# First 42 expert blocks of the first PEER pass: both activation parts in one 512-column matmul, their sum on VectorE, and the gate stage nine blocks later

## The chip, the cores and the metric

The kernel runs on one core of a Trainium2 chip. The metric is the device time of one launch in microseconds (us); lower is better. Three runs of the kernel before gave 1034.63, 1034.99 and 1036.53 us, median 1034.99. In the text PE is TensorE (PEld its weight loads), DVE is VectorE, ACT is ScalarE, POOL is GpSimd and SP is the engine that issues the weight DMAs.

## The reference, cut to what matters

One decoder layer for 256 tokens and a model width of 1024: attention in two head groups, then PEER, a retrieval of 16 of 128 x 128 single-neuron experts per head for 8 heads, and a final norm. The change touches PEER alone:

```python
s1, s2 = q1 @ keys1, q2 @ keys2                 # (T, 8, 128) each
v1, i1 = top_k(s1, 16); v2, i2 = top_k(s2, 16)
cand = v1[..., :, None] + v2[..., None, :]      # 16 x 16 sums per head
sc, ci = top_k(cand, 16)
e = i1[ci // 16] * 128 + i2[ci % 16]            # which experts
g = softmax(sc)
act = gelu(hc @ exp_u[e])                       # hc: (T, 1024)
out = (g * act) @ exp_v[e]
```

The kernel computes it densely: gelu(h · u) for all 16384 experts in 128 blocks of 128 experts, each multiplied by a gate that is zero for experts that weren't chosen, and then the product with all of v.

## The kernel before

**Split numbers.** Each fp32 factor is split into a high part that the matmul takes exactly and a low part, the rest. A product takes three of the four combinations: high·high, high·rest, low·high. `h2r[:, 0]` holds the high part of the activations h (128 rows, 8 chunks of the contraction, 256 tokens) and `h2r[:, 1]` the rest; the weights of a block are `hi_t` and `lo_t`.

**The first pass (u pass).** `u_block(n)`, for n from 0 to 127, computes 128 experts by 256 tokens in half a PSUM bank, banks 4 and 5 in turn. For each of 8 chunks two matmuls of 256 columns take the same weights `hi_t` with both activation parts (L875, L876); then 8 matmuls of 256 columns take `lo_t` with the high part (L879). A block so has 24 matmuls of 256 columns. The second pass (v pass, L899 and L906) has 12 matmuls of 512 columns a block.

**Who feeds a block.** SP loads block n into one of 5 raw buffers once block n-5 is done. ACT copies it into `hi_t` (L591, 3 buffers, so not before block n-3 is done). The low part is raw minus high: on POOL for n below `POOL_LOW` = 46 (L434), on DVE from there on (L1231). ACT also takes the gelu of the finished block from PSUM (L612 or L610). ACT's order in the loop is `high(n + 1)`, then `gelu(n - 1)`: so `high(k + 3)` stands right behind `gelu(k)`, and an engine runs its instructions in the order in which they are written. Block n+2 waits for the gelu of block n to free its bank.

**The sort.** While PE runs the first 46 blocks, DVE finds the 16 best of each list. For each of two tiles of 128 tokens: `top16` over 16 lists of 128 scores (MAX8 L1185, FIND_INDEX8 L1188, MATCH_REPLACE8 L1192, and again for the next 8), the candidate sums (L1203), `top16` over 8 lists of 256, the difference to the best (L1207, after which ACT may take the exponential, at its step `EXP_AT` = 38), and twice a comparison, a product and a reduction over 2048 columns, `hit` and `chosen` (L1217, L1219, L1221), which look the chosen indices up. Then come the gate sums and `chosen_ready` (L1226).

**The gates.** Before block `TURN_AT` = 46 PE waits for `chosen_ready` and transposes the choices (L934). From block `GATE_AT` = 52 on, each of 64 blocks is preceded by the matmuls that build the gates of 4 tokens (L890, 8 matmuls) out of one-hot rows that DVE makes (L1242 to L1248). DVE multiplies them into the activations of all blocks done so far (L1259), ACT keeps the rest of them for the blocks to come (L619), and `late` (L1267) multiplies these in later. The last gates so stand ahead of block 115, and 12 blocks without gates follow before the v pass.

## Time and profile before

| | before |
|---|---|
| median of 3 runs | 1034.99 us |
| profiled execution | 1034.67 us, its span 1032.9 us |
| u pass on PE | 266.4 to 674.1 us |
| PE, DVE, ACT, POOL busy | 93%, 72%, 47%, 27% of the span |
| granted TensorE clock | 0.973 of full speed over the span |

The span runs from the first instruction to the last; some 1.8 us of the execution lie outside it. The groups further down come from the page, from the chain that ended last (each piece follows the one that released it), from the instructions of an engine in order of time (start, duration, engine and line, result and operands with shapes, count, and in brackets the idle time before and who ended it), and from stretches of time with each engine's busy time. Two instructions on an engine overlap by some 0.07 us where the second needs nothing of the first, so durations of neighbours add up to a little more than the time between starts.

### The profile page before, as it was taken

The page shows a single profiled execution, that of the slowest core. Times are in us where ns is not written, and L with a number is a line of the kernel's source. Part 1 is how long each engine was busy: PE and PEld are TensorE (multiplying, and loading weights), DVE is VectorE, ACT ScalarE, POOL GpSimd, SP SyncE. Part 2 cuts the span into 40 slices and gives each one's busy share as a digit, 9 for nine tenths or more (in the row PEclk, how much of TensorE's full clock was granted, in tenths as well). Part 3 has the DMA queues.
Part 4 walks back from the last instruction along what each step waited for, and adds up shares of the span by engine and source line. Part 5 has one row for each costly group of instructions (what it writes and reads, how often), then busy time and mean ns, then how long its engine had stood idle before and what let it go on. Part 6 is the DMA issues. An engine that isn't in the chain of part 4 may idle for free.

```text
span 1032.9 us, 16975 instructions
## 1 busy us (share of the span) xinstructions
PE 960.8 (93%) x6674; PEld 881.5 (85%) x6674; DVE 740.6 (72%) x1358; ACT 486.9 (47%) x865; POOL 278.7 (27%) x138
## 2 busy tenths in 40 slices
PE   2299898699999999999999999999999999999996
PEld 2198778698999999999999999988888888888884
DVE  4935869870699998789999998555555555555555
ACT  5355435332644454454444444454545454545453
POOL 5566446656799995000000000000000000000000
PEclk9599999899999999999999999999999999999998
DMA  9994457612365665554545545666666666666662
GB/s 291 285 363 168 164 202 328 265 62 103 102 184 165 183 184 165 164 160 149 163 149 158 156 152 164 184 183 195 193 195 193 195 192 193 194 193 195 193 194 102
DMA packets 58162, 191.60 MB, mean 186 GB/s; under 512 B 4946, under 2 KB 23522, under 8 KB 56932
## 3 DMA queue, kind: packets, MB, share of 16 engines
q1 hardware_dynamic: 58018, 190.50, 57.3%
q8 instruction: 53, 0.87, 0.4%
q14 instruction: 25, 0.20, 0.1%
q0 software_dynamic: 64, 0.03, 0.0%
q10 hardware_dynamic: 2, 0.00, 0.0%
HBM read 189.44 MB, written 1.07 MB: 184 GB/s over the span
## 4 chain that ended last, share of the span: by engine, by line
PE 82%; DVE 9%; POOL 4%; ACT 2%; issue 1%; DMA 1%; SPq 0%; DVEq 0%; ACTq 0%
PE banks L899 22%; PE banks L906 11%; PE banks L875 11%; PE banks L879 11%; PE banks L876 10%; PE banks L720 5%; DVE acc L962 5%; POOL lo L434 4%; PE banks L890 3%; PE banks L729 2%; PE banks L717 1%; DMA sc_w<-in_w_ada 1%; PE banks L726 1%; DVE prob L1085 1%; PE banks L857 1%
## 5 line engine op out<-in xcount | busy, mean ns | idle before, releaser
L1231 DVE TENSOR_TENSOR lo<-raw,hi 128x1024 fp32r<-128x1024 f32 x210 | 258.9, 1233 | 169.7 <-ACT hi L591 168.3
L591 ACT ACTIVATE hi<-raw 128x1024 fp32r<-128x1024 f32 x256 | 271.5, 1061 | 169.7 <-PE banks L906 169.7
L875 PE MATMUL banks<-h2r,hi 128*128 128x256 f32 x1024 | 256.4, 288 | 0.0
L899 PE MATMUL banks<-hi,wsplit 128*128 128x512 f32 x1024 | 253.2, 389 | 0.5 <-DVE wsplit L1272 0.5
L876 PE MATMUL banks<-h2r,hi 128*128 128x256 f32 x1024 | 251.1, 283 | 0.0
L899 PEld LDWEIGHTS banks<-hi,wsplit 128*128 128x128 f32 x1024 | 192.2, 188 | 40.5 <-issue 0.7
L876 PEld LDWEIGHTS banks<-h2r,hi 128*128 128x128 f32 x1024 | 196.6, 192 | 0.0
L875 PEld LDWEIGHTS banks<-h2r,hi 128*128 128x128 f32 x1024 | 196.0, 191 | 0.0
L879 PE MATMUL banks<-h2r,lo 128*128 128x256 f32 x1024 | 143.9, 283 | 3.4 <-POOL lo L434 3.4
L906 PE MATMUL banks<-lo,wsplit 128*128 128x512 f32 x512 | 137.0, 389 | 0.0
L879 PEld LDWEIGHTS banks<-h2r,lo 128*128 128x128 f32 x1024 | 132.0, 192 | 4.2 <-POOL lo L434 4.2
L434 POOL TENSOR_TENSOR lo<-raw,hi 128x1024 fp32r<-128x1024 f32 x46 | 129.4, 2836 | 20.5 <-ACT hi L591 20.1
L906 PEld LDWEIGHTS banks<-lo,wsplit 128*128 128x128 f32 x512 | 96.1, 188 | 19.9
L610 ACT ACTIVATE gelu_out<-banks 128x256 f32<-128x256 f32 (+32 forms) x75 | 22.1, 295 | 131.7 <-PE banks L879 131.7
L612 ACT ACTIVATE act<-banks 128x256 f32<-128x256 f32 (+31 forms) x116 | 37.4, 323 | 84.1 <-PE banks L879 84.1
L427 POOL TENSOR_TENSOR win_low<-win,high 128x1024 fp32r<-128x1024 f32 x24 | 59.3, 2494 | 40.1 <-ACT high L462 40.1
L1272 DVE TENSOR_TENSOR wsplit<-act,wsplit 128x256 fp32r<-128x256 f32 x128 | 53.4, 417 | 0.4 <-ACT wsplit L631 0.4
L631 ACT ACTIVATE wsplit<-act 128x256 fp32r<-128x256 f32 x128 | 51.2, 400 | 0.0
L1248 DVE TENSOR_TENSOR oh2g<-oh,part_h 128x512 f16<-128x512 f16 x128 | 48.2, 417 | 0.0
L427 POOL TENSOR_TENSOR wq_low<-wq,high 128x1024 fp32r<-128x1024 f32 x16 | 40.7, 2575 | 23.0 <-ACT high L462 23.0
L962 DVE SCALAR_TENSOR_TENSOR acc<-sc_w,cact,acc 128x256 f32<-128x256 f32 (+1 forms) x35 | 39.9, 1141 | 1.1
L890 PE MATMUL banks<-oh2g,oh 128*128 128x128 f16 x512 | 40.6, 220 | 0.0
(171 smaller groups left out, 1057.8 us busy)
## 6 DMA issues: line engine op xcount, KB each, us to landing
raw<-in_u_t SPq DMA_DIRECT2D x128, 512.0 KB, 3.6
raw<-in_v_b SPq DMA_DIRECT2D x128, 512.0 KB, 3.8
win<-in_w_in SPq DMA_DIRECT2D x8, 1024.0 KB, 11.9
g_w<-in_w_ada SPq DMA_DIRECT2D x2, 4096.0 KB, 14.3
wq<-in_wq SPq DMA_DIRECT2D x2, 4096.0 KB, 13.7
sh_w<-in_w_ada SPq DMA_DIRECT2D x4, 1024.0 KB, 11.9
sc_w<-in_w_ada SPq DMA_DIRECT2D x4, 1024.0 KB, 12.1
win<-in_w_in SPq DMA_DIRECT2D x1, 4096.0 KB, 19.1
```

Of the source, the lines that this page charges most:

```text
L427: nc.gpsimd.tensor_tensor(low_of[name][:, :, c], full[name][:, :, c], high_slot(w)[:, :, e * P:(e + 1) * P].bitcast(F32), ALU.subtract).th ...
L434: nc.gpsimd.tensor_tensor(lo_t[n % RAW][:, :], raw[n % RAW][:, :], hi_t[:, n % HI, :].bitcast(F32), ALU.subtract).then_inc(pool_low, 1)
L591: nc.scalar.activation(hi_t[:, n % HI, :], raw[n % RAW][:, :], ACT.Copy).then_inc(high_ready, 1)
L875: nc.tensor.matmul(dst, w, h2r[:, 0, c, :], start=(c == 0), stop=False)
L876: nc.tensor.matmul(dst, w, h2r[:, 1, c, :], start=False, stop=False)
L879: last = nc.tensor.matmul(dst, lo_t[n % RAW][:, c * P:(c + 1) * P], h2r[:, 0, c, :], start=False, stop=(c == DC - 1))
L890: last = nc.tensor.matmul(bank[g_bank(g)][:, k * KEYS:(k + 1) * KEYS], oh1[:, g % 2, k // PT, :, k % PT], oh2g[:, g % 2, e, k // PT, :, k ...
L899: nc.tensor.matmul(bank[2 * t + half][:, :], wsplit[:, j % WS, e, t * P:(t + 1) * P], hi_t[:, n % HI, half * 512:half * 512 + 512], start= ...
L906: last = nc.tensor.matmul(bank[2 * t + half][:, :], wsplit[:, j % WS, 0, t * P:(t + 1) * P], lo_t[n % RAW][:, half * 512:half * 512 + 512] ...
L962: ins = nc.vector.scalar_tensor_tensor(out=dst, in0=w[:, c, :], scalar=cact[:, c:c + 1], in1=dst, op0=ALU.mult, op1=ALU.add)
L1231: nc.vector.tensor_tensor(lo_t[n % RAW][:, :], raw[n % RAW][:, :], hi_t[:, n % HI, :].bitcast(F32), ALU.subtract).then_inc(vector_low, 1)
L1272: nc.vector.tensor_tensor(wsplit[:, j % WS, 1, :], act[:, j, :], wsplit[:, j % WS, 0, :].bitcast(F32), ALU.subtract).then_inc(wl_ready, 1)
```

## The change

For the first `MERGED` = 42 blocks, the two matmuls of 256 columns with the same weights become one of 512 columns: the high products go into columns 0 to 255 of a bank and the products with the rest into columns 256 to 511. The low weights still add to columns 0 to 255. A DVE `tensor_reduce` adds the two halves of a block into `u_sum` (two buffers, in SBUF), and ACT takes the gelu from there; it waits for this sum (`summed`) where it waited for the block. Four banks take the blocks in turn, so that block n waits for the sum of block n-4. The sum of block n waits for the block and for the gelu of block n-2.

The sums stand inside DVE's sort at fixed places. `weave` adds up the sort's lengths by numbers in the code (0.2, 0.27, 0.33, 0.4, 2.3, 2.4 and 4.4 us for its instructions, 0.65 for a sum) and puts sum k in as soon as the total is over 3.0 · (k + 1.4). `EXP_AT` goes from 38 to 45, `POOL_LOW` and `TURN_AT` from 46 to 55 (POOL makes nine more low parts and DVE nine fewer) and `GATE_AT` from 52 to 61, so that the last gates stand ahead of block 124.

```diff
-EXP_AT = 38
-POOL_LOW = 46
-TURN_AT = 46
-GATE_AT = 52
+EXP_AT = 45
+POOL_LOW = 55
+TURN_AT = 55
+GATE_AT = 61
+MERGED = 42
...
+        def u_bank(n):
+            return (4, 5, 0, 1)[n % 4] if n < MERGED else 4 + n % 2
...
             def gelu(n):
                 before = gated_before(n)
+                if n < MERGED:
+                    sc.wait_ge(summed, n + 1)
+                    nc.scalar.activation(act[:, n, :], u_sum[:, n % 2, :], ACT.Gelu).then_inc(act_out, 1)
+                    return
                 sc.wait_ge(block_used, n + 1)
...
             def u_block(n):
                 pe.wait_ge(high_ready, n + 1)
-                if n >= 2:
-                    pe.wait_ge(act_out, n - 1)
+                if n < MERGED:
+                    if n == 2:
+                        pe.wait_ge(rows_read, 3)
+                    if n >= 4:
+                        pe.wait_ge(summed, n - 3)
+                    for c in range(DC):
+                        nc.tensor.matmul(bank[u_bank(n)].rearrange("p (e s) -> p e s", e=2),
+                                         hi_t[:, n % HI, c * P:(c + 1) * P], h2r[:, :, c, :],
+                                         start=(c == 0), stop=False, skip_group_check=True)
+                    low_ready(n)
+                    for c in range(DC):
+                        last = nc.tensor.matmul(bank[u_bank(n)][:, 0:SEQ], lo_t[n % RAW][:, c * P:(c + 1) * P],
+                                                h2r[:, 0, c, :], start=False, stop=(c == DC - 1), skip_group_check=True)
+                    last.then_inc(block_used, 1)
+                    return
+                pe.wait_ge(act_out, n - 1)
...
+            SLOT = 3.0
+            sorted_for, added = [0.0], [0]
+            def add_parts(n):
+                ve.wait_ge(block_used, n + 1)
+                if n >= 2:
+                    ve.wait_ge(act_out, n - 1)
+                nc.vector.tensor_reduce(u_sum[:, n % 2, :], bank[u_bank(n)].rearrange("p (e s) -> p s e", e=2), AX.X,
+                                        ALU.add).then_inc(summed, 1)
+            def weave(length):
+                sorted_for[0] += length
+                while added[0] < MERGED and SLOT * (added[0] + 1.4) < sorted_for[0]:
+                    add_parts(added[0])
+                    added[0] += 1
+                    sorted_for[0] += 0.65
...
                         last = nc.vector.max(vals[:, l, k:k + 8], src(l))
+                        if l < n - 1:
+                            weave(one)
...
                     link(nc.vector.tensor_tensor(hit[:, :, :, :], hit[:, :, :, :],
                                                  spread(halves_i[:, half], 2, TOPK), ALU.mult))
+                    weave(4.4)
                     link(nc.vector.tensor_reduce(chosen[:, t, half, :], hit[:, :, :, :], AX.X, ALU.add))
+                    weave(2.3)
```

On PE, in the fourth and fifth block (n = 3 and 4), the order of the changed kernel is this (L887 takes `hi_t`, L892 takes `lo_t`):

```order
337 L887 MATMUL banks<-h2r,hi 128x512 [waits high_ready]
338 L887 MATMUL banks<-h2r,hi 128x512 x7
339 L892 MATMUL banks<-h2r,lo_107 128x256 [waits pool_low]
340 L892 MATMUL banks<-h2r,lo_107 128x256 x7
341 L887 MATMUL banks<-h2r,hi 128x512 [waits summed,high_ready]
342 L887 MATMUL banks<-h2r,hi 128x512 x7
343 L892 MATMUL banks<-h2r,lo_108 128x256 [waits pool_low]
344 L892 MATMUL banks<-h2r,lo_108 128x256 x7
```

A block has 16 matmuls in place of 24, and from n = 4 on it waits for a sum. On DVE, the last part of the second tile's sort, from the comparison on, before:

```order
187 L1217 TENSOR_TENSOR hit<-part,iota 128x2048
188 L1219 TENSOR_TENSOR hit<-hit,top_i 128x2048
189 L1221 TENSOR_REDUCE chosen<-hit 128x128
190 L1217 TENSOR_TENSOR hit<-part,iota 128x2048
191 L1219 TENSOR_TENSOR hit<-hit,top_i 128x2048
192 L1221 TENSOR_REDUCE chosen<-hit 128x128
```

And the same part in the changed kernel, where L1214 is the sum of a block's halves, L1270 the comparison, L1273 the product and L1276 the reduction:

```order
249 L1270 TENSOR_TENSOR hit<-part,iota 128x2048
250 L1214 TENSOR_REDUCE u_sum<-banks 128x256 x2
251 L1273 TENSOR_TENSOR hit<-hit,top_i 128x2048
252 L1214 TENSOR_REDUCE u_sum<-banks 128x256
253 L1276 TENSOR_REDUCE chosen<-hit 128x128
254 L1270 TENSOR_TENSOR hit<-part,iota 128x2048
255 L1273 TENSOR_TENSOR hit<-hit,top_i 128x2048
256 L1276 TENSOR_REDUCE chosen<-hit 128x128
```

These three sums are the last ones, of blocks 39, 40 and 41: the last sum stands four long instructions ahead of the sort's end. At the start of the sort the first sums stand here (L1229 is MAX8, L1234 FIND_INDEX8):

```order
149 L1229 MAX top_v<-score 128x8 x16
150 L1234 MAX_INDEX top_iu<-top_v,score 128x8 x5
151 L1214 TENSOR_REDUCE u_sum<-banks 128x256
152 L1234 MAX_INDEX top_iu<-top_v,score 128x8 x9
153 L1214 TENSOR_REDUCE u_sum<-banks 128x256
```

Before, the 16 searches for indices stood there without a break.

## Rows read from the trace of the kernel before

**Rows 1.** The page: busy time by engine, chain that ended last by engine.

```profile
PE 960.8 (93%) x6674; PEld 881.5 (85%) x6674; DVE 740.6 (72%) x1358; ACT 486.9 (47%) x865; POOL 278.7 (27%) x138
...
PE 82%; DVE 9%; POOL 4%; ACT 2%; issue 1%; DMA 1%; SPq 0%; DVEq 0%; ACTq 0%
```

**Rows 2.** The chain in order of time (start us, us, what), 255 to 480 us.

```profile
268.56 0.96 PE banks L879 x8
...
271.44 0.96 PE banks L879 x8
...
373.97 19.66 POOL lo L434 x5
...
402.56 0.96 PE banks L879 x8
403.52 0.66 PE banks L934 x6
...
421.44 0.48 PE banks L890 x8
```

**Rows 3.** The chain on PE in the second pass, 674 to 690 us.

```profile
677.14 1.81 PE banks L899 x8
678.95 0.91 PE banks L906 x4
```

**Rows 4.** DVE's instructions in order of time (start us, us, engine, line), first tile's sort.

```profile
267.10 3.19 DVE L1185 MAX8 top_v<-score 128x8 f32<-128x128 f32 x16 [18.04 <-ACT score L596]
270.32 0.09 DVE L1188 MATCH_VALUE_LOAD top_iu<-top_v,score 128x8 f32 x1
...
286.48 1.44 DVE L1200 CAST top_i<-top_iu 128x256 f32<-128x256 uint32 x1
...
305.65 2.43 DVE L1207 TENSOR_TENSOR gate<-best 128x128 f32<-128x128 f32 x1
```

**Rows 5.** The same, last part of the second tile's sort.

```profile
371.39 4.38 DVE L1217 TENSOR_TENSOR hit<-part,iota 128x2048 f32<-128x2048 f32 x1
375.80 4.39 DVE L1219 TENSOR_TENSOR hit<-hit,top_i 128x2048 f32<-128x2048 f32 x1
380.23 2.29 DVE L1221 TENSOR_REDUCE chosen<-hit 128x128 f32<-128x2048 f32 x1
...
391.42 2.29 DVE L1221 TENSOR_REDUCE chosen<-hit 128x128 f32<-128x2048 f32 x1
```

**Rows 6.** DVE groups by shape (busy us, mean ns): reduce of two kinds.

```profile
L1221 DVE TENSOR_REDUCE chosen<-hit 128x128 f32<-128x2048 f32 x4 | 9.1, 2286 | 0.1
...
L1073 DVE TENSOR_REDUCE nmax<-logit 128x2 f32<-128x512 f32 x8 | 5.5, 686 | 0.3
```

**Rows 7.** DVE in order of time, late in the gate window.

```profile
629.86 0.62 DVE L1259 TENSOR_TENSOR act<-banks,act 128x452 f32<-128x452 f32 x1
630.41 1.23 DVE L1231 TENSOR_TENSOR lo<-raw,hi 128x1024 fp32r<-128x1024 f32 x1
...
633.26 0.62 DVE L1259 TENSOR_TENSOR act<-banks,act 128x456 f32<-128x456 f32 x1
```

**Rows 8.** ACT in order of time, from the first block.

```profile
269.56 0.38 ACT L612 ACTIVATE act<-banks 128x256 f32<-128x256 f32 x1 [1.06 <-PE banks L879]
269.84 1.05 ACT L591 ACTIVATE hi<-raw 128x1024 fp32r<-128x1024 f32 x1
```

**Rows 9.** POOL in order of time.

```profile
305.53 2.40 POOL L434 TENSOR_TENSOR lo<-raw,hi 128x1024 fp32r<-128x1024 f32 x1 [0.48 <-ACT hi L591]
```

**Rows 10.** PE in order of time, after the first tile's hit products.

```profile
330.99 1.22 PE L879 MATMUL banks<-h2r,lo 128*128 128x256 f32 x8 [1.25 <-POOL lo L434]
```

**Rows 11.** PE in order of time, its longest wait in the attention stage.

```profile
117.04 0.61 PE L778 MATMUL banks<-ident,prob 128*128 128x128 f32 x2 [4.04 <-DVE prob L1085]
```

**Rows 12.** Stretches: busy us (count) of each engine, then PEclk, DMA share, GB/s.

```profile
112.00:118.00 6.00, 1.96 (x15) 1.43 (x13) 5.89 (x6) 1.93 (x2) 6.00 (x3) 0.93 1.10 437
118.00:122.00 4.00, 4.00 (x26) 3.78 (x25) 3.96 (x4) 0.95 (x5) 1.19 (x1) 0.68 0.91 393
```

More of the change, by code:

```diff
@@ L153, in hybrid_peer_layer @@
         gelu_out = at("gelu_out", M0 + 1024, [P, 2, SEQ])
+        u_sum = at("u_sum", M0 + 1024, [P, 2, SEQ])
         iota_t = at("iota_t", M0, [P, GQ, KEYS, PT], F16)
@@ L239, in hybrid_peer_layer @@
             sem, ("second_ready", "onehot_ready", "gates_ready", "gates_used", "gates_out"))
+        summed = sem("summed")
         wh_ready, wl_ready, peer_ready, x2_ready, final_ready = map(
@@ L1178, in _, with top16 @@
                                     None, ALU.mult).then_inc(rows_read, 1)
-            def top16(vals, idx, src, n):
+            SLOT = 3.0
[12 more added lines that the diff above has]
+                    sorted_for[0] += 0.65
+            def top16(vals, idx, src, n, one):
                 for k in range(0, TOPK, 8):
@@ L1188, in top16 @@
                         last = nc.vector.max_index(idx[:, l, k:k + 8], vals[:, l, k:k + 8], src(l))
+                        if l < n - 1:
+                            weave(one + 0.07)
                     link(last)
@@ L1192, in top16 @@
                             last = nc.vector.match_replace(src(l), vals[:, l, k:k + 8], src(l), -3.0e38)
+                            if l < n - 1:
+                                weave(one + 0.07)
                         link(last)
@@ L1198, in _ @@
                     ve.wait_ge(s_ready, TT * LISTS // 4)
-                top16(top_v, top_iu, lambda l: score[:, t, l, :], LISTS)
+                top16(top_v, top_iu, lambda l: score[:, t, l, :], LISTS, 0.2)
                 link(nc.vector.tensor_copy(top_i[:, :, :], top_iu[:, :, :]))
@@ L1204, in _ @@
                                              spread(halves_v[:, 1], 2, TOPK), ALU.add))
-                top16(best, best_iu, lambda h: cand[:, h, :, :].rearrange("p a b -> p (a b)"), HEADS)
+                weave(2.3)
+                top16(best, best_iu, lambda h: cand[:, h, :, :].rearrange("p a b -> p (a b)"), HEADS, 0.33)
                 nc.vector.tensor_tensor(gate[:, t, :, :], best[:, :, :],
@@ L1209, in _ @@
                                         ).then_inc(gate_max, 1)
+                assert added[0] <= EXP_AT
+                weave(2.4)
                 nc.vector.tensor_scalar(part_u[:, 0, :, :], best_iu[:, :, :], 4, None, ALU.logical_shift_right)
@@ L1218, in _ @@
                                                  ALU.is_equal))
+                    weave(4.4)
                     link(nc.vector.tensor_tensor(hit[:, :, :, :], hit[:, :, :, :],
                                                  spread(halves_i[:, half], 2, TOPK), ALU.mult))
+                    weave(4.4)
                     link(nc.vector.tensor_reduce(chosen[:, t, half, :], hit[:, :, :, :], AX.X, ALU.add))
+                    weave(2.3)
             ve.wait_ge(gate_exp, TT)
@@ L1275, in _ @@
             low(POOL_LOW)
+            assert added[0] == MERGED, added
             low(POOL_LOW + 1)
```

## The prediction

> **What bounds the kernel now.** I read the page first. PE is busy 93% of the span, and 82% of the chain that ended last is PE [rows 1]: whatever shortens or stops PE shows in the time. Then the chain in order of time. In the u pass the low products of two blocks start at 268.56 and 271.44, so a block takes 2.88 us, and its 8 low matmuls take 0.96 us, 0.12 us each [rows 2]; 16 high ones are 1.92 us. Block 0 ends at 269.52 (268.56 + 0.96) and block 45, the last before the transposes, at 403.52. These are 134.0 us for 45 blocks, where 45 x 2.88 = 129.6: PE lost 4.4 us. The chain says to whom: five of POOL's low parts from 373.97 on took 19.66 us, 3.93 each [rows 2], while one of them usually takes 2.40 [rows 9]; PE's wait at 330.99 is the end of the earlier such period [rows 10]. Last, DVE in order of time tells why. A product of 2048 columns with both inputs in SBUF takes 4.4 us beside a busy POOL, the gate difference of only 128 columns 2.43 us and a cast of 256 columns 1.44 [rows 4, 5]: such an instruction and POOL's take turns, some 2.2 us of waiting for each other and 2.2 of work. A reduction of 2048 columns takes 2.29 us in the same stretch [rows 5], so it does not take part in the turns.
>
> The Trainium skill says the same of this pair in "SBUF — State Buffer", section "Who interferes with whom": a tensor_tensor with two SBUF inputs shuts GpSimd out of a shared port for its whole length and the other way round, and on trn2 a tensor_reduce never does; by that rule, with which the trace agrees, the 42 new sums cost POOL nothing.
>
> **What the change saves on PE.** In the v pass 8 matmuls of 512 columns take 1.81 us, 0.227 each [rows 3], against 0.240 for two of 256. A merged block is 1.81 + 0.96 = 2.77 us in place of 2.88. For 42 blocks that is 42 x 0.11 = 4.6 us, if nothing else holds a block up.
>
> "TensorE: Matmul & The Clock Gate", section "Wait — 56ns, not 53.3ns?", of the Trainium skill puts a warm matmul at its columns over 2.4 GHz and 2.5 ns; by that the merge would save 0.02 us a block, 0.9 us in all. The trace's 0.120 and 0.227 are both above it, and the rows give the larger gain.
>
> **What it adds on DVE.** 42 sums, each reading 512 columns of PSUM. A reduction of 512 columns took 0.686 us, and one of 2048 took 2.29, so it is the columns read that count [rows 6]. A PSUM read with a stride, 452 columns, took 0.62, and the next instruction started 0.55 after it [rows 7]: neighbours overlap by 0.07. So a sum takes 0.62 of DVE's time and ends 0.69 after its start. Bounds: 0.55, that row's distance, and 1.10, if the alternating halves went at the pace of L1217, 4.38 us for 2048 columns [rows 5]. I take 0.62, since both nearer rows stand there. 42 sums make 26 us on an engine that had no pause in the sort.
>
> **Where this lands.** The sums stand at fixed places of the sort, so DVE's progress through the sort now sets when a block is released. Behind the sum of block k stand in a row: its gelu (the copy after it starts 0.28 later), ACT's copy for block k+3 (1.05) [rows 8], and POOL's low part of k+3 (2.40) [rows 9]; 3.8 us with the hand-overs. Block k+3 wants its low part 2 x 2.77 + 1.81 = 7.35 us after the end of block k. The sum may thus end 3.5 us after its block; later than that, PE waits. The wait for the sum of block n-4 is looser by a block and never decides.
>
> Sum 0 stands behind 16 MAX8, done at 270.32 [rows 4], and five searches, so it starts over 2 us after block 0. Sum 39 stands behind the comparison that ended at 371.39 + 4.38 = 375.77 [rows 5]. With 39 sums ahead of it, 39 x 0.62 = 24.2, it ends at 375.77 + 24.2 + 0.69 = 400.6. From the first to the 39th that is about (400.6 - 270.3) / 40 = 3.3 us a sum, where a block used to take 2.88 and would take 2.77. PE uses up its 3.5 us in some three blocks and then goes at DVE's pace. The gain of 4.6 us so lies beside a wait and is worth nothing here; the 4.4 us that were lost to POOL lie inside the new waits too.
>
> Now the walk from sum 39 at 400.6, by the order of instructions:
> - gelu 39, then ACT's copy 42 until 402.0. DVE does sum 40 and then finds the port free (POOL waits for the copy): product 401.3 to 403.45.
> - POOL's low part 42 from 403.45 to 405.85, block 42 ends 0.96 + 0.1 later, 406.9. Sum 41 is done at 404.1, the reduction at 406.4.
> - low part 43 until 408.25; block 43 (unmerged again) ends at 409.8.
> - DVE's third comparison takes the port from 408.25 to 410.4, low part 44 until 412.8, block 44 ends at 413.8.
> - the last product 412.8 to 414.95, low part 45 until 417.35, block 45 ends at 418.3.
>
> Before, block 45 ended at 403.52 [rows 2]: **14.8 us later**. From there each block takes 2.88 as before.
>
> Three corrections to DVE's stream ahead of sum 39:
> - *DVE waits for PE.* Where long instructions stand (cast and candidates; gate difference and comparison, in both tiles) some 7 us pass between sums, and PE falls back by about 4 us. The next sums stand in pairs or close together, but their blocks aren't done: DVE waits. An engine that is late for its partner in one stretch and early in the next loses on both sides. Four such places, half a block (1.25) lost at each: +5.0. Bounds 0 and a block at each, 11.
> - *Port time given back.* POOL, held up by PE's pace, is now busy 44 x 2.40 = 106 of some 135 us, 78%. The part of DVE's waits for it that falls away is 22% of 16.5 us (five products and comparisons at 2.2, two gate differences at 2.2, a cast at 1.1 [rows 4, 5]): -3.6. Bounds 0 and -16.5.
> - *PE's clock.* In the kernel before, PE waited 4.04 us at one place [rows 11]; the granted clock was 0.93 of full speed in the 6 us around it and 0.68 in the next four [rows 12], which is 4 x 0.32 = 1.3 us of full-speed work. In the u pass it was never paused that long. The four new pauses of about 4 us are of this size; I count one of them, +1.3. Bounds 0 and 5.2.
>
> **What the rest costs.** The exponential at ACT's step 45 stands where the kernel before had it at 38, behind a value that DVE has long made; it delays copies that have 3.5 us to spare: 0, up to 2. POOL's nine more low parts replace DVE's: 0 on PE, since 2.40 fits in 2.88. `chosen_ready` comes some 5 us after the sort, near 422, and the transposes now stand ahead of block 55, at 418.3 + 9 x 2.88 = 444: no wait. The 64 gate groups are the same (8 matmuls in 0.48 [rows 2]). But their last ones now meet longer rows: DVE's round between two gate products was 3.40 us (629.86 to 633.26 [rows 7]), which is PE's 2.88 + 0.48 and the hand-over, with DVE full; 36 more columns add 0.04 a round for the last seven, and only three blocks follow instead of twelve before the v pass needs wsplit: +0.3, between 0 and 2.
>
> Sum: 14.8 + 5.0 - 3.6 + 1.3 + 0.3 = 17.8. On the profiled execution, 1034.67, that makes 1052.5 us; the median of the runs is 0.3 above this execution, which I leave in the range.
>
> **The rivals.**
> - *PE sets the pace after all (faster).* One mechanism: DVE's sort with its sums keeps within 3.5 us of the blocks, and the merge pays. For it: the numbers of the weave ask for 3.0 us a sum, near a block. Against it: these leave out the cast's and the link instructions' time and DVE's stream, summed from rows, runs at 3.3. It needs the stream ahead of sum 39 shorter by some 18 us, more than all of DVE's waits for the port. Price: -4.6, 1030.1 us. By the skill's matmul times quoted above it would be 1033.8.
> - *The port is given back nearly whole.* POOL idles whenever DVE asks. -16.5 for -3.6: 1039.6; half of it, 1046. For it: POOL will always wait for ACT's copy. Against it: it also must catch up after each pause, just when DVE's long products stand.
> - *The clock falls at each pause.* 3 x 1.3 more and waits of DVE behind it: 1056 to 1062. For it: the one wait of 4.04 us. Against: PE's pause is broken by the high products, which start before the low part is there.
> - *Nothing changes*, because savings on PE and port cancel the pace: 1035. It would need sum 39 near 385.
>
> **How the numbers follow.** The forecast holds 0.70, for 1047 to 1058; the clock 0.12; the port 0.11; faster 0.05; no change 0.02. The likeliest gives 1052.5. For 8 in 10 the range takes in the forecast's own, half of the port's rival and most of the clock's: 1045 to 1061. A sum at 1.10 us, 20 us more, is left outside. What a measurement can tell from no change is 0.2%, 2 us: faster 0.05, within 0.02, slower 0.93.
>
> **What would show it.** The profile after should show: 16 matmuls a block, 0.227 and 0.120 us; sums of 0.69; ACT's gelu waiting for DVE in most of the first 42 blocks; PE waiting for ACT's copy or POOL's low part near the casts and products, some 20 us in all; block 41 done near 404 to 408 and block 45 near 418 to 421; v pass unchanged but 18 us later. I am wrong if the gelus find their sums ready, if the waits lie at the turn to the v pass, or if a sum takes the time of L1217.

## The result, and the profile after

| | before | after |
|---|---|---|
| median (range), the same chip | 1035.76 us (1034.63 to 1038.09, 4 runs) | 1055.10 us (1054.90 to 1055.73, 4 runs) |
| profiled execution, its span | 1034.67, 1032.9 | 1055.28, 1053.5 |
| first matmul of the u pass to first of the v pass | 266.41 to 674.13: 407.7 | 268.04 to 694.72: 426.7 |
| granted clock over the span | 0.973 | 0.965 |

The ratio is 1.0185, 95% interval 1.0165 to 1.0204: 1.9% slower, clear of no change. The u pass is 19.0 us longer. The other 1.6 us between the two spans lie ahead of the u pass, and the experiments show starts between 266.3 and 268.7 whatever the edit, so they are not the change's. Two lines of the page, busy time and the chain by engine, answer to [rows 1]:

```profile
PE 967.8 (92%) x6338; PEld 869.3 (83%) x6338; DVE 750.1 (71%) x1382; ACT 486.2 (46%) x865; POOL 291.5 (28%) x147
...
PE 72%; DVE 19%; POOL 3%; ACT 2%; issue 2%; DMA 1%; SPq 0%; DVEq 0%; ACTq 0%
```

DVE's busy time grew by only 9.5 us, but its share of the chain went from 9% to 19%: it did not become full, it is waited for. The v pass kept its length (its high matmuls start from 674.1 to 1021.7 us before, from 694.7 to 1042.3 after). Here are PE's instructions of the u pass that come after its longer waits (start, duration, what, idle before and who ended it):

```profile
297.85 3.78 PE L887 MATMUL banks<-h2r,hi 128*128 128x512 f32 x8 [3.38 <-ACT hi L598]
325.55 2.14 PE L887 MATMUL banks<-h2r,hi 128*128 128x512 f32 x8 [2.43 <-ACT hi L598]
329.17 1.22 PE L892 MATMUL banks<-h2r,lo 128*128 128x256 f32 x8 [1.49 <-POOL lo L441]
...
379.99 2.11 PE L887 MATMUL banks<-h2r,hi 128*128 128x512 f32 x8 [3.00 <-ACT hi L598]
408.50 0.35 PE L900 MATMUL banks<-h2r,hi 128*128 128x256 f32 x1 [3.61 <-ACT act L613]
422.89 1.22 PE L904 MATMUL banks<-h2r,lo 128*128 128x256 f32 x8 [1.24 <-POOL lo L441]
```

All 13 waits from 266 to 430 add up to 18.3 us; before, there were four of 3.4 us in all, one of them in [rows 10]. The first matmuls after a wait tell the clock: 8 of 512 columns took 3.78 us at 297.85, and 2.14 and 2.11 at the next two such places. The stretches (the columns are those of [rows 12]) show where full speed was lost:

```profile
291.00:314.00 23.00, 19.54 (x95) 16.47 (x95) 22.49 (x72) 8.10 (x12) 15.56 (x7) 0.85 0.43 129
314.00:344.00 30.00, 25.75 (x143) 21.46 (x141) 26.91 (x26) 12.54 (x20) 24.11 (x9) 1.00 0.54 157
...
394.00:423.00 29.00, 22.90 (x146) 20.28 (x146) 28.69 (x29) 13.93 (x22) 22.48 (x9) 0.94 0.43 140
```

That is 23 x 0.15 + 29 x 0.06 = 5.2 us of full-speed work; about 0.5 of it lies in the pause ahead of 297.85, whose last 0.95 us already had the lower clock (0.50 granted from 296.90 on). The chain that ended last, in the stretch that answers to [rows 2], no longer runs over PE's own matmuls but over DVE's instructions, a copy of ACT and POOL's low parts:

```profile
403.63 2.30 DVE hit L1270
...
405.96 0.70 DVE u_sum L1214
...
407.00 1.05 ACT hi L598
...
408.12 14.72 POOL lo L441 x4
```

The groups of the new sums, and of the gelus behind them (busy us, mean ns, idle before and until whom), answer to [rows 6, 8]:

```profile
L1214 DVE TENSOR_REDUCE u_sum<-banks 128x256 f32<-128x512 f32 x42 | 28.3, 680 | 5.9 <-PE banks L892 4.9 <-DVE chosen L1276 0.7
L613 ACT ACTIVATE act<-u_sum 128x256 f32<-128x256 f32 x42 | 17.5, 417 | 84.5 <-DVE u_sum L1214 84.5
```

Both directions of the coupling stand there: ACT waited 84.5 us for sums, and DVE in turn 4.9 us for blocks. Nearly all of the 4.9 lies at two sums:

```profile
330.43 0.69 DVE L1214 TENSOR_REDUCE u_sum<-banks 128x256 f32<-128x512 f32 x1 [2.81 <-PE banks L892]
...
349.10 0.69 DVE L1214 TENSOR_REDUCE u_sum<-banks 128x256 f32<-128x512 f32 x1 [1.84 <-PE banks L892]
```

Last, DVE in order of time, the instructions beside the sums, which answer to [rows 4, 5]:

```profile
291.70 1.65 DVE L1250 CAST top_i<-top_iu 128x256 f32<-128x256 uint32 x1
...
315.62 0.29 DVE L1258 TENSOR_TENSOR gate<-best 128x128 f32<-128x128 f32 x1
315.83 0.68 DVE L1214 TENSOR_REDUCE u_sum<-banks 128x256 f32<-128x512 f32 x1
316.43 1.93 DVE L1263 TENSOR_SCALAR part_u<-best_iu 128x128 uint32<-128x128 uint32 x1
318.29 2.44 DVE L1264 TENSOR_SCALAR part_u<-best_iu 128x128 uint32<-128x128 uint32 x1
...
321.08 2.29 DVE L1270 TENSOR_TENSOR hit<-part,iota 128x2048 f32<-128x2048 f32 x1
...
324.62 2.28 DVE L1273 TENSOR_TENSOR hit<-hit,top_i 128x2048 f32<-128x2048 f32 x1
...
333.96 4.41 DVE L1270 TENSOR_TENSOR hit<-part,iota 128x2048 f32<-128x2048 f32 x1
...
339.60 3.17 DVE L1273 TENSOR_TENSOR hit<-hit,top_i 128x2048 f32<-128x2048 f32 x1
...
373.08 2.42 DVE L1250 CAST top_i<-top_iu 128x256 f32<-128x256 uint32 x1
...
397.39 0.62 DVE L1258 TENSOR_TENSOR gate<-best 128x128 f32<-128x128 f32 x1
...
398.54 2.38 DVE L1263 TENSOR_SCALAR part_u<-best_iu 128x128 uint32<-128x128 uint32 x1
400.84 2.43 DVE L1264 TENSOR_SCALAR part_u<-best_iu 128x128 uint32<-128x128 uint32 x1
```

Four long instructions of the first tile that took 4.4 us before now take between 2.28 and 4.41, but in each tile two small ones of 128 columns, which follow a sum, take 1.9 to 2.4. In the kernel before, the same two and the second tile's cast read:

```profile
308.00 0.21 DVE L1210 TENSOR_SCALAR part_u<-best_iu 128x128 uint32<-128x128 uint32 x1
308.13 0.21 DVE L1211 TENSOR_SCALAR part_u<-best_iu 128x128 uint32<-128x128 uint32 x1
...
350.43 0.29 DVE L1200 CAST top_i<-top_iu 128x256 f32<-128x256 uint32 x1
...
368.45 2.31 DVE L1207 TENSOR_TENSOR gate<-best 128x128 f32<-128x128 f32 x1
```

### The profile page after: what moved, and what is told of

It reads as the page before. It is cut to its first block, busy times and chain, and to the rows that moved or that the text cites. A ratio compares the mean times of both kernels' runs of the same rounds, so it can differ in the third digit from the quotient of the medians.

```text
span 1053.5 us, 16356 instructions
## 1 busy us (share of the span) xinstructions
PE 967.8 (92%) x6338; PEld 869.3 (83%) x6338; DVE 750.1 (71%) x1382; ACT 486.2 (46%) x865; POOL 291.5 (28%) x147
## 4 chain that ended last, share of the span: by engine, by line
PE 72%; DVE 19%; POOL 3%; ACT 2%; issue 2%; DMA 1%; SPq 0%; DVEq 0%; ACTq 0%
PE banks L924 22%; PE banks L931 11%; PE banks L900 8%; PE banks L904 7%; PE banks L901 7%; PE banks L731 5%; DVE acc L987 5%; POOL lo L441 3%; PE banks L915 3%; PE banks L740 2%; DVE u_sum L1214 2%; DVE top_iu L1234 2%; PE banks L728 1%; DMA sc_w<-in_w_ada 1%; DVE top_v L1229 1%
## 5 line engine op out<-in xcount | busy, mean ns | idle before, releaser
L1287 DVE TENSOR_TENSOR lo<-raw,hi 128x1024 fp32r<-128x1024 f32 x201 | 246.2, 1225 | 182.0 <-ACT hi L598 180.5
L900 PE MATMUL banks<-h2r,hi 128*128 128x256 f32 x688 | 174.6, 292 | 3.6 <-ACT act L613 3.6
L901 PE MATMUL banks<-h2r,hi 128*128 128x256 f32 x688 | 169.3, 284 | 0.0
L441 POOL TENSOR_TENSOR lo<-raw,hi 128x1024 fp32r<-128x1024 f32 x55 | 141.6, 2595 | 51.0 <-ACT hi L598 51.0
L900 PEld LDWEIGHTS banks<-h2r,hi 128*128 128x128 f32 x688 | 132.0, 192 | 3.8 <-ACT hi L598 3.8
L901 PEld LDWEIGHTS banks<-h2r,hi 128*128 128x128 f32 x688 | 132.5, 193 | 0.0
L887 PE MATMUL banks<-h2r,hi 128*128 128x512 f32 x336 | 86.5, 400 | 8.8 <-ACT hi L598 8.8
L904 PEld LDWEIGHTS banks<-h2r,lo 128*128 128x128 f32 x688 | 89.2, 193 | 2.5 <-POOL lo L441 2.5
L887 PEld LDWEIGHTS banks<-h2r,hi 128*128 128x128 f32 x336 | 61.7, 193 | 20.6 <-ACT hi L598 9.4
L621 ACT ACTIVATE gelu_out<-banks 128x4 f32<-128x4 f32 (+32 forms) x66 | 18.7, 283 | 119.6 <-PE banks L904 119.6
L613 ACT ACTIVATE act<-u_sum 128x256 f32<-128x256 f32 x42 | 17.5, 417 | 84.5 <-DVE u_sum L1214 84.5
L892 PEld LDWEIGHTS banks<-h2r,lo 128*128 128x128 f32 x336 | 45.7, 193 | 11.4 <-POOL lo L441 8.9
L892 PE MATMUL banks<-h2r,lo 128*128 128x256 f32 x336 | 48.8, 289 | 4.3 <-POOL lo L441 4.1
## 6 DMA issues: line engine op xcount, KB each, us to landing
g_w<-in_w_ada SPq DMA_DIRECT2D x2, 4096.0 KB, 15.2
```

What stands on the lines that cost most here:

```text
L441: nc.gpsimd.tensor_tensor(lo_t[n % RAW][:, :], raw[n % RAW][:, :], hi_t[:, n % HI, :].bitcast(F32), ALU.subtract).then_inc(pool_low, 1)
L887: nc.tensor.matmul(bank[u_bank(n)].rearrange("p (e s) -> p e s", e=2), hi_t[:, n % HI, c * P:(c + 1) * P], h2r[:, :, c, :], start=(c == 0) ...
L892: last = nc.tensor.matmul(bank[u_bank(n)][:, 0:SEQ], lo_t[n % RAW][:, c * P:(c + 1) * P], h2r[:, 0, c, :], start=False, stop=(c == DC - 1) ...
L900: nc.tensor.matmul(dst, w, h2r[:, 0, c, :], start=(c == 0), stop=False)
L901: nc.tensor.matmul(dst, w, h2r[:, 1, c, :], start=False, stop=False)
L904: last = nc.tensor.matmul(dst, lo_t[n % RAW][:, c * P:(c + 1) * P], h2r[:, 0, c, :], start=False, stop=(c == DC - 1))
```

## The experiments

Each kernel ran beside the kernel before on its chip; the medians of before there were 1035.6 (n1 to n3, n5), 1035.5 (n4, n6 to n8), 1035.0 (n9 to n11) and 1035.1 us (n12). "u pass" is the distance between the first matmuls of the two passes: 407.7 before, 426.7 after.

| run | median us | ratio to before, 95% | u pass |
|---|---|---|---|
| n1 constants alone | 1036.1 | 0.9990 to 1.0013 | 407.7 |
| n2 merged, no sums | 1033.7 | 0.9969 to 0.9989 | 405.6 |
| n3 sums of half the columns | 1046.0 | 1.0082 to 1.0119 | 418.0 |
| n4 sums every 2.7 | 1041.9 | 1.0041 to 1.0071 | 414.4 |
| n5 copy ahead of gelu | 1049.9 | 1.0120 to 1.0162 | 421.6 |
| n6 both of these | 1037.1 | 1.0001 to 1.0021 | 409.0 |
| n7 also true lengths, 36 merged | 1034.8 | 0.9986 to 1.0003 | 407.4 |
| n8 DVE's load, nobody waits | 1032.8 | 0.9953 to 0.9977 | 404.8 |
| n9 before, lookup in PSUM | 1030.4 | 0.9948 to 0.9973 | 403.3 |
| n10 merged, lookup in PSUM | 1038.9 | 1.0028 to 1.0059 | 411.5 |
| n11 after, lookup in PSUM | 1050.3 | 1.0131 to 1.0160 | 423.6 |
| n12 n10 with sums every 2.5 | 1029.1 | 0.9923 to 0.9948 | 400.7 |

Two single executions stand far out, 1597 us in n6 and 3331 us of the kernel before beside n12; nothing on record explains them, and the medians don't hang on them.

**n1, the four constants alone.** The kernel before with only this part of the change:

```diff
-EXP_AT = 38
-POOL_LOW = 46
-TURN_AT = 46
-GATE_AT = 52
+EXP_AT = 45
+POOL_LOW = 55
+TURN_AT = 55
+GATE_AT = 61
```

> The kernel before with only the four numbers of the change: the exponential at step 45, POOL's low parts and the transposes up to block 55, the gates from block 61. No merged matmuls and no sums. My theory (the loss is DVE's pace in the sort) puts these at +0.3 us, 0 to 2: 1036.1 us, v pass starting 0 to 0.5 us later than in the kernel before. Rival: the later gates run into the turn to the v pass, or POOL's nine more low parts hold PE up; then this run shows 5 us or more of the 19, with PE waits near the last gates or in blocks 46 to 55.

The u pass kept its 407.7 us and the median is within what can be told. The later gates and POOL's nine more low parts cost nothing; all of the loss is in the merged blocks.

**n2, merged without sums.** The gelu reads the high half straight from the bank, so the product with the activations' rest is left out for 42 blocks:

```diff
-                    sc.wait_ge(summed, n + 1)
-                    nc.scalar.activation(act[:, n, :], u_sum[:, n % 2, :], ACT.Gelu).then_inc(act_out, 1)
+                    sc.wait_ge(block_used, n + 1)
+                    nc.scalar.activation(act[:, n, :], bank[u_bank(n)][:, 0:SEQ], ACT.Gelu).then_inc(act_out, 1)
...
-                        pe.wait_ge(summed, n - 3)
+                        pe.wait_ge(act_out, n - 3)
...
-                    add_parts(added[0])
```

> The changed kernel without DVE's sums: the gelu of the first 42 blocks reads the high half of the bank and waits for the block as before; the products with the rest of the activations are made but not added. My theory: PE then runs 42 blocks at 2.77 us and the time is the kernel before's less 42 x 0.11 = 4.6 plus 0.3 for the constants: 1031.5 us, with the two periods of POOL's slow low parts (4.4 us) as before or up to 1.5 us larger, since PE is faster. Rival: 512-column matmuls over two halves cost what the sums seem to cost (weights or PSUM): then it stays above 1040.

Half of the gain that I expected: the u pass is 2.1 us shorter, not 4.3. The chain in order of time shows why the first half is smaller:

```profile
268.15 1.85 PE banks L887 x8
269.99 0.95 PE banks L892 x8
270.95 1.84 PE banks L887 x8
```

A merged block takes 2.79 us, 0.230 a matmul, so 42 of them save 3.8. Most of the rest is POOL: PE's four waits for it, of 0.90, 1.32, 0.81 and 1.25 us, remain (4.3 us with 3.4 before), and two more blocks were held up by 0.3 each. I take it that a quicker PE runs into POOL's slow periods earlier; no run shows that by itself.

**n8, DVE's load without the coupling.** n2 with 42 reductions of the same size and at the same places, but of columns in SBUF that are long ready, and nobody waits for them:

```diff
-                ve.wait_ge(block_used, n + 1)
-                    ve.wait_ge(act_out, n - 1)
-                nc.vector.tensor_reduce(u_sum[:, n % 2, :], bank[u_bank(n)].rearrange("p (e s) -> p s e", e=2), AX.X,
+                    ve.wait_ge(summed, n - 1)
+                nc.vector.tensor_reduce(u_sum[:, n % 2, :], xs[:, 0, 0:512].rearrange("p (e s) -> p s e", e=2), AX.X,
```

> The changed kernel with 42 reductions of 512 columns on DVE at the same places, but of columns in SBUF that are ready, waiting for no block, and with nobody waiting for them; the gelu takes the high half of the bank as in the kernel without sums (the products with the rest of the activations are not added). DVE's load as in the changed kernel, the coupling gone. Theory (coupling): the sort ends some 25 us later, near 424, still ahead of the transposes near 440: 1033.7, up to 1 more. Rival (DVE's load itself, by the port it shares with POOL or the late choice): 1040 or more.

42 reductions of 696 ns on DVE, 29 us, cost nothing. What costs in the changed kernel is not DVE's time, but that PE must wait for the place at which a sum stands. These reductions read SBUF, so the run doesn't test whether reads of the PSUM banks cost anything; n12 does, with 42 such reads and a single wait of PE, 0.75 us.

**n3, half of a sum's columns.** The sum covers 128 of 256 tokens, and the gelu uses it for both halves (the others' product is left out):

```diff
-                nc.vector.tensor_reduce(u_sum[:, n % 2, :], bank[u_bank(n)].rearrange("p (e s) -> p s e", e=2), AX.X,
+                nc.vector.tensor_reduce(u_sum[:, n % 2, 0:P], bank[u_bank(n)].rearrange("p (e s) -> p s e", e=2)[:, 0:P, :], AX.X,
```

> The changed kernel with each sum over 128 of the 256 tokens, at the same place; the gelu takes these for both halves of the tokens, so the output of the other half is not computed. A sum takes 0.33 us of DVE's time in place of 0.60. Theory of DVE's stream: 42 x 0.27 = 11 us less work ahead of the last sum, of which DVE's waits for PE give back a part: 8 to 11 us faster than the changed kernel, 1044 to 1047. Rival (the long instructions between two sums and the chain behind a sum make the loss, not the sums' own time): 0 to 3 us faster, 1052 to 1055.

A sum took 0.412 us instead of 0.680, 11.3 us less in 42, and the u pass fell by 8.7 us: the time follows DVE's stream, less what DVE then waits more for PE (8.3 us in place of 4.9).

**n4, the sums closer together.** The sums stand at the same work, earlier in the sort:

```diff
-            SLOT = 3.0
+            SLOT = 2.7
-                while added[0] < MERGED and SLOT * (added[0] + 1.4) < sorted_for[0]:
+                while added[0] < MERGED and SLOT * (added[0] + 1.1) < sorted_for[0]:
```

> The changed kernel with the sums placed closer: sum k at 2.7 (k + 1.1) of the sort's counted length in place of 3.0 (k + 1.4). The same 42 sums, the same ACT order. Theory (what counts is how much sort stands ahead of each sum): the last sum has 13.5 us of counted sort less ahead of it, DVE waits a little more for PE in exchange: 7 to 12 us faster than the changed kernel, 1043 to 1048. Rival (the number of sums, or DVE's load, sets the loss): 1054 to 1056.

12.3 us less for two numbers, without any work removed; the median, 1041.9, is 1.1 us below the range that I gave. The pauses that ACT's copy ended are 1.00, 0.93 and 1.04 us long, and the clock is at full speed behind them:

```profile
298.26 2.12 PE L887 MATMUL banks<-h2r,hi 128*128 128x512 f32 x8 [1.00 <-ACT hi L598]
...
385.26 2.10 PE L887 MATMUL banks<-h2r,hi 128*128 128x512 f32 x8 [1.04 <-ACT hi L598]
```

Of the 6.7 us that n4 still loses against the kernel before, only 2.8 stand at the end of block 45. The others lie behind it, where the last lookups now meet POOL's low parts and PE waited for POOL three times (1.13, 0.74 and 1.25 us).

**n5, ACT's copy ahead of the gelu.** `high(k + 3)` stands ahead of `gelu(k)`, so a late sum doesn't hold up the copy behind it:

```diff
-                if HI <= n + 1 < STREAM:
-                    high(n + 1)
+                ahead = n + 2 if n <= MERGED else n + 1
+                if HI <= ahead < STREAM and n != MERGED + 1:
+                    high(ahead)
```

> The changed kernel with ACT's copy for block k+3 ahead of the gelu of block k for the first 42 blocks, so that a late sum no longer holds the copy and POOL's low part; a sum then holds PE only through its bank, a block and the chain's 3.8 us later. Theory: the pauses at the four places with long instructions shrink from about 4 us to 1 or less, but DVE's stream still brings the last sum to 402 to 405: 4 to 8 us faster than the changed kernel, 1047 to 1051. If DVE's stream alone were the bound, and the order on ACT did nothing: 1055. If the chain behind the sum alone were: back to 1035 or below.

5.1 us shorter, as expected in size; the pauses did only half of what I expected. The slack of a sum grew, and two of them shrank, from 3.38 and 3.00 us to 1.61 and 0.19. But the second one grew from 2.43 to 3.22, and with DVE's stream nearly as long as before, PE met it at the end of the merged blocks:

```profile
404.42 0.55 PE L901 MATMUL banks<-h2r,hi 128*128 128x256 f32 x1 [6.36 <-ACT act L613]
```

**n6, n4 and n5 together.**

> Both at once: ACT's copy for block k+3 ahead of gelu k, and the sums at 2.7 (k + 1.1). Theory: the two act on different parts, the placing on DVE's stream, the order on the pauses at the long instructions, so most of both adds up: 1036 to 1041. PE's pauses should be under 2 us each. Rival (both remove the same wait): no better than the better of the two alone, 1043 to 1050.

The u pass is 409.0 us, 17.7 less than after, where the two alone gave 12.3 and 5.1: they add up. One makes the sums come faster, the other widens the time that PE can do without one.

**n7, and with the true lengths.** n6 with the cast's and the small instructions' time counted in the weave, 0.61 for a sum and 36 merged blocks:

```diff
                 link(nc.vector.tensor_copy(top_i[:, :, :], top_iu[:, :, :]))
+                weave(1.5)
...
                 link(nc.vector.tensor_copy(part[:, :, :, :], part_u[:, :, :, :]))
+                weave(0.8)
...
-                    sorted_for[0] += 0.65
+                    sorted_for[0] += 0.61
-MERGED = 42
+MERGED = 36
```

> The previous edit, with the sort's lengths counted as the trace has them (1.5 for the cast and 0.8 for the three small ones that the weave leaves out, 0.61 for a sum) and 36 merged blocks in place of 42, so that the last sums stand ahead of the second tile's long products. Theory: a sum then comes within what its block can wait for, and the time falls to that of the kernel without sums (1033.7) plus at most 3: 1033.5 to 1036.5, same as the kernel before or just faster. Rival (some wait for DVE remains at each long instruction whatever the placing): 1038 or more.

All of the loss is gone, and of the gain 0.4 us show. At the end of block 45 the whole gain of 36 merged blocks was there: 133.87 us from the first matmul, 3.25 less than before, with waits of 0.31 (ACT's copy), 1.51 and 1.31 us (POOL) left. Behind it 2.9 us went again, as in n4: PE waited for POOL 0.73 and 1.25 us. The lengths and the number of blocks changed together, so their shares are not shown.

**n9, the lookup in PSUM, on the kernel before.** The comparison's result goes to PSUM banks, and the positions `part` too, so that no lookup has two inputs in SBUF:

```diff
+        hit_p = banks[:, 0:4, :].rearrange("p b (h k j) -> p (b h) k j", h=2, k=TOPK)
+        part_p = bank[7][:, 0:2 * HK].rearrange("p (a h k) -> p a h k", a=2, h=HEADS)
...
-                    link(nc.vector.tensor_tensor(hit[:, :, :, :], spread(part[:, half], 3, TOPK), place,
+                    link(nc.vector.tensor_tensor(hit_p, spread(part_p[:, half], 3, TOPK), place,
```

> The kernel before, with the comparison and product of the index lookup in PSUM: hit in banks 0 to 3 and the positions in bank 7, so that neither instruction has both inputs in SBUF. Nothing else changes. Theory of turns (two SBUF inputs take turns with POOL): each of the eight falls from 4.4 to about 2.3 us, POOL's low parts stay at 2.4 beside them, PE's two periods of waiting (4.4 us in all) go, 1031.3 us for 1035.5, and the sort ends some 17 us earlier without effect. Rival (the instructions are long by themselves, or POOL is slowed by any DVE work): 4.4 us each as before and 1035.5.

DVE in order of time, the first tile's comparison and product, and one of POOL's low parts beside them:

```profile
308.76 2.30 DVE L1220 TENSOR_TENSOR banks<-banks,iota 128x2048 f32<-128x2048 f32 x1
311.10 2.30 DVE L1222 TENSOR_TENSOR banks<-banks,top_i 128x2048 f32<-128x2048 f32 x1
...
311.21 2.40 POOL L436 TENSOR_TENSOR lo<-raw,hi 128x1024 fp32r<-128x1024 f32 x1 [0.48 <-ACT hi L593]
```

2.30 us in place of 4.4 [rows 5], and PE waited for nobody in the whole sort: the 4.4 us that the u pass lost are won back (403.3 for 407.7). The turns that the prediction read out of the 4.4 us are shown: they go, on both sides, when one input and the result leave SBUF. It is not that PSUM is quicker: with everything in SBUF, but started in a pause of POOL's, the same instruction took 2.28 and 2.29 us (324.62 and 321.08 after). Which of the two, the input or the result, frees it, this run doesn't separate. The Trainium skill, "SBUF — State Buffer", section "Who interferes with whom", puts it down to the inputs: outside the modes that use both ports, a DVE instruction with at most one SBUF input does not contend with GpSimd.

**n11, the lookup in PSUM, on the changed kernel.** The same edit, with three banks (4, 5, 6) for the merged blocks, so that block n waits for the sum of block n-3.

> The changed kernel with the lookup in PSUM and nothing else (banks 4, 5 and 6 for the merged blocks; sums where they stood, by the old lengths). Theory: with the eight lookups at 2.3 in place of up to 4.4 us and no turns there, DVE's stream ahead of the last sum is 8 to 12 us shorter and POOL's low parts behind it are not held up: 1038 to 1044. The pause at the cast and the candidates of each tile stays. Rival (the pauses come from the placing alone): 1052 or more.

Missed: 1050.3 us where I expected 1038 to 1044, and not the rival's 1052 either; the u pass is 3.1 us shorter, where I expected 8 to 12 of DVE's stream alone. The lookups fell to 2.30, but the small instructions ahead of them did not, and the pauses stayed at their places:

```profile
314.88 1.93 DVE L1266 TENSOR_SCALAR part_u<-best_iu 128x128 uint32<-128x128 uint32 x1
316.73 2.44 DVE L1267 TENSOR_SCALAR part_u<-best_iu 128x128 uint32<-128x128 uint32 x1
```

```profile
296.31 3.78 PE L889 MATMUL banks<-h2r,hi 128*128 128x512 f32 x8 [3.39 <-ACT hi L600]
...
376.57 3.59 PE L889 MATMUL banks<-h2r,hi 128*128 128x512 f32 x8 [2.98 <-ACT hi L600]
```

Only five lookups stand ahead of sum 39, and after the change they held just 3.0 us of waiting (2.29, 2.28, 4.41, 3.17, 2.29 against 2.29 each). That is the most that n11 could give back ahead of sum 39. The sum ended 1.8 us earlier, as DVE waited 0.9 us more for PE, and another 1.3 came behind it. I had priced the lookups with the 4.4 us of the kernel before.

**n10, all of it.** Copy first, true lengths, lookup in PSUM, 42 merged blocks in three banks, sums every 2.8.

> The merged blocks (42) with all that the runs so far point to: ACT's copy ahead of the gelu, sums at 2.8 (k + 1.1) of lengths counted as they are without the turns, and the lookup in PSUM as in the run before (the merged blocks then take turns in banks 4, 5 and 6). Theory: PE loses neither the 4.4 us to POOL nor more than 1 to the sums, and keeps the merge's 42 x 0.09 = 3.8: 1027 to 1030. Rival (every sum has some cost on PE, through ACT or the banks): no better than the lookup in PSUM alone, 1031 to 1033.

Missed by at least 8.9 us. PE waited for sums through the banks:

```profile
361.82 2.09 PE L890 MATMUL banks<-h2r,hi 128*128 128x512 f32 x8 [1.54 <-DVE u_sum L1217]
...
387.88 2.09 PE L890 MATMUL banks<-h2r,hi 128*128 128x512 f32 x8 [1.88 <-DVE u_sum L1217]
...
394.19 0.55 PE L903 MATMUL banks<-h2r,hi 128*128 128x256 f32 x1 [3.27 <-ACT act L615]
```

Three banks look like the culprit. But the first and last sum start at 270.7 and 395.8, so they come 3.05 us apart on average, and DVE itself had idled only 0.5 us ahead of them. Two causes were open, the banks and DVE's spacing.

**n12, the same with one number changed,** `SLOT` from 2.8 to 2.5.

> The kernel of n10 with one number changed: the sums are woven in every 2.5 us of counted DVE time instead of 2.8 (42 merged blocks, lookup in PSUM, three banks). In n10 the blocks came every 3.04 us, ACT waited for a sum at all 42 gelus, and DVE never waited for PE. If DVE's spacing set that pace (my theory), the spacing falls to about 3.04 x 2.5/2.8 = 2.71, under the block's 2.79, DVE now waits for PE, and the u pass takes some 403 to 407 us instead of 411.5: a median of 1030 to 1035 us. If it is the three banks in place of four (PE waits for the sum of block n-3), the pace stays and the time is 1037 or more.

It was the spacing: the sums come every 2.84 us, with the same three banks. The first line below is PE's only wait in the sort; then stand the groups of the sums and gelus:

```profile
387.06 0.36 PE L903 MATMUL banks<-h2r,hi 128*128 128x256 f32 x1 [0.75 <-ACT act L615]
```

```profile
L1217 DVE TENSOR_REDUCE u_sum<-banks 128x256 f32<-128x512 f32 x42 | 28.5, 683 | 2.2 <-PE banks L895 1.6
L615 ACT ACTIVATE act<-u_sum 128x256 f32<-128x256 f32 x42 | 17.3, 411 | 30.4 <-DVE u_sum L1217 30.3
```

ACT now waits for 21 of the sums instead of all 42, as DVE waits for PE at some. 1029.1 us is the fastest of all: 0.5 to 0.8% under before, 26 us under the changed kernel, with the same matmuls, the same 42 sums and the same four constants. Against n9, which has the lookup in PSUM and no merged blocks, the u pass is 2.6 us shorter: about the merge's 3.8 less that wait and its restart. So most of n12's gain is the lookup's, and the merge adds little; the two intervals against before, 0.9923 to 0.9948 and 0.9948 to 0.9973, just touch.

## Why the prediction was right, and where its terms were off

The forecast of 1052.5 us missed by 2.6. Direction, mechanism and PE's pauses were right; two of the terms were not, and one that came out right did so by luck. Times below count from the first matmul of the u pass, 266.41 before and 268.04 after.

| step | predicted us | measured us |
|---|---|---|
| merged block | 2.77, 42 save 4.6 | 2.79, 42 save 3.8 |
| a sum | 0.62, ends after 0.69 | 0.60, ends after 0.68 |
| DVE waits ahead of sum 39 | 5.0 | 5.6 (4.9 of it for PE) |
| port time given back | 3.6 | 0.6 |
| end of sum 39 | 135.6 | 138.6 |
| from there to the end of block 45 | 17.7 | 17.5 |
| the clock as a term of its own | 1.3 | 0 to 0.3 |
| after block 45 | 0.3 | 0 |
| the u pass longer by | 17.8 | 19.0 |

**The walk from sum 39 held.** Its chain (gelu, ACT's copy, POOL's low parts in turn with DVE's products) took 17.5 us. In it block 42 had to wait for gelu 40 and not just for a low part, 3.61 us, since its bank must be free; the low parts behind it took their turns as worked out, the last one with 4.38 for the product. The end of block 45 and the whole u pass both came 19.0 us later, so nothing was lost or won behind it, as n1 shows from the other side. On the span's own clock block 45 ended at 424.1, past the 418 to 421 that were named as a sign; 1.6 of this is the later start of the u pass.

**PE's four pauses** stand where the prediction put them, by the cast and the gate difference of both tiles, 2.43 to 3.61 us long, where it said about 4. From PE's side the same 19.0 add up: block 45 ended 156.1 us after the start, where 42 x 2.79 + 4 x 2.88 = 128.7 would do, so 27.4 were lost: 18.3 of waits, 5.2 of clock, and 3.9 that are left for 13 restarts, 0.3 each (4.4 if the 0.5 us of clock inside a pause is not counted twice). Before it was 137.1 - 132.5 = 4.6, with four waits of 3.4 in all, which leaves 0.3 for each restart there too. 27.4 - 4.6 - 3.8 = 19.0.

**DVE's waits came out right by luck.** I counted half a block at each of four places in both tiles, 5.0 us. The trace has 5.6, but nearly all of it behind the first tile's gate difference: 2.81 us at 330.43 and 1.84 at 349.10 for PE, and 0.68 at 346.37 that was not for PE. There were 0.27 us behind the first tile's cast (303.38), and none in the second tile ahead of sum 39.

**The port's term failed, by 3.0 us.** I said that POOL idles 22% of the time and DVE so gets 22% of its waits back. Beyond their time alone (0.29 for casts and the gate difference, 0.21, 2.29), the contended instructions ahead of sum 39 held 15.8 us before (1.15 for a cast, 4.16 for two gate differences, 10.5 for five lookups). After: 3.5 for casts, 0.3 for gate differences, 3.0 for lookups, and 8.3 for four small instructions that had cost nothing. That is 15.2. POOL in order of time shows how:

```profile
312.52 2.40 POOL L441 TENSOR_TENSOR lo<-raw,hi 128x1024 fp32r<-128x1024 f32 x1 [1.06 <-ACT hi L598]
315.87 4.76 POOL L441 TENSOR_TENSOR lo<-raw,hi 128x1024 fp32r<-128x1024 f32 x2 [0.96 <-ACT hi L598]
```

Before, the gate difference waited for POOL and the two small instructions behind it ran in POOL's pause. Now the gate difference (315.62) found a pause, a sum stands behind it, POOL started meanwhile, and the small instructions end at 318.3 and 320.7, one behind each of POOL's two. One wait became two. I had taken the waits as a share of POOL's time; they hang on what starts first. n11 agrees with the size of the lookups' part, 3.0 us and not the 10.5 of the kernel before.

**The clock** fell at two of the four pauses, not one (3.78 us for 8 matmuls at 297.85, and 0.94 of full speed in the last stretch). That is 5.2 us of PE's speed, but hardly a term of its own in the end, since PE was the one who waited. Behind the first fall DVE waited 0.27 us for PE (303.38), which is the most that it can have cost; behind the second the chain ran over POOL's low parts (408.12 to 422.84) and not over PE.

**Of the rivals** none held. "PE sets the pace" failed here since DVE's stream came at 3.3 us a sum. Its price was too high as well: n2, where without sums PE does set the pace for all 42 blocks, took 1033.7 us and not 1030.1, because a block saves 0.09 and not 0.11 us and POOL's waits grow. n7 holds the pace with its sums in place and gives most of the gain back behind block 45. Only n12, where POOL's waits are gone too, gets below 1030.1. The clock's rival counted on a fall at each pause; it fell at two, and the time stayed below its 1056. (A small slip: the 0.9 us that the prediction sets beside its own 4.6 is 0.8 by its own 0.02 a block.)

What stays open: why a restart costs 0.3 us, and what a version of n12 with four banks would give, which wasn't tried.

## What to carry to other kernels

Work that another engine waits for, woven into an in-order stream, costs by the spacing at which it comes. Its duration counts only as a part of that spacing: 29 us of reductions cost nothing where nobody waited (n8), and halving them where PE did wait gave 8.7 us (n3). The same 42 sums cost 19 us at a counted spacing of 3.0, 7 at 2.7 (n4), and one wait of 0.75 us at 2.5, with ACT's copy first, truer lengths and the port freed (n12). Sum the stream from the trace, with small instructions and port waits (2.8 counted was 3.05 real in n10), and set the spacing so that the weaving engine sometimes waits for its partner rather than the other way round. And order the consumer's queue so that nobody else's input stands behind the late item (n5, n6).

## What the runs showed of the hardware

- A small instruction can carry a whole port wait. A TENSOR_SCALAR of 128 columns took 0.21 us in POOL's pause and 1.93 to 2.44 beside it, a cast of 256 columns 0.29 and 2.42. The Trainium skill, "SBUF — State Buffer", section "Who interferes with whom", says that casts and tensor_scalar can take a mode that needs the shared port; these rows agree. With one input and the result in PSUM a tensor_tensor of 2048 columns was free of it, 2.30 for 4.4 (n9), and the sums of 512 columns kept 0.67 to 0.69 us in every run that has them whole.
- The length of a pause does not tell alone whether the clock falls. In the changed kernel it fell after waits of 3.38 and 3.61 and held after 2.43 and 3.00; in n11, 2.74 and 2.98 brought it down (3.59 us for 8 matmuls behind the latter), and so did one of 2.54 in n3:

```profile
294.97 3.37 PE L888 MATMUL banks<-h2r,hi 128*128 128x512 f32 x8 [2.54 <-ACT hi L598]
```

The shortest is in n4: behind a wait of 2.23 us the granted clock was 0.57 of full speed from 325 to 329 us.

```profile
324.06 1.21 PE L892 MATMUL banks<-h2r,lo 128*128 128x256 f32 x8 [2.23 <-POOL lo L441]
325.11 3.34 PE L887 MATMUL banks<-h2r,hi 128*128 128x512 f32 x8
```
